# A hybrid decoder layer in split float32: queries in 512-column products, and layer norm by transposed moments

## The reference

```python
h = rmsnorm(x, g_mix[l]); proj = h @ w_in[l]          # 1024 x 4608
q, k, v = ...                                         # 8 heads of 64
u = proj[..., c_v:c_u] + b_glu[l]                     # 2 x 512 channels
o = moba_attention(q, k, v)                           # causal softmax, 256 keys
a, g = split(u); z = a * sigmoid(g)
z = depthwise_conv(z, w_dw, 31 taps) + b_dw           # 512 channels, causal
z = (z - mean(z)) * rsqrt(var(z) + EPS)               # over the 512 channels of a token
cz = silu(z * ln_g + ln_b)
merged = gate_a * (o @ w_attn_up[l]) + gate_c * (cz @ w_conv_pw[l] + b_conv_pw[l])
x = x + merged @ w_out[l]
h = rmsnorm(x, g_ffn[l])
x = x + square(relu(h @ w_ff1[l])) @ w_ff2[l]; return rmsnorm(x, g_final)
```

## Time and profile before

| | |
|---|---|
| median of three runs | 351.67 us |
| span of the profiled execution, first to last instruction | 350.3 us |
| TensorE busy | 344.2 us (98%) |
| TensorE weight loads | 289.5 us (83%) |
| VectorE busy | 251.5 us (72%) |
| ScalarE busy | 192.1 us (55%) |
| GpSimd busy | 3.5 us |
| read from memory | 63.0 MB, 183 GB/s over the span |

### The profile page before, as it was taken

How to read it: one execution, slowest core, us unless ns; L and a number is a source line. 1 busy time by engine, 2 the same in 40 slices (tenths; PEclk the granted TensorE clock), 3 DMA queues, 4 the chain that set the end, 5 groups by cost and what they waited for, 6 DMA issues and landing times.

```text
span 350.3 us, 4670 instructions
## 1 busy us (share of the span) xinstructions
PE 344.2 (98%) x1766; PEld 289.5 (83%) x1766; DVE 251.5 (72%) x313; ACT 192.1 (55%) x236; POOL 3.5 (1%) x13
## 2 busy tenths in 40 slices
PE   8999999999999999999999999999999999999994
PEld 5889988787778888888888888888888888889884
DVE  2969999899999889965666946639466394563813
ACT  4985644698796358434674535515355163551534
POOL 1000000000000000000000000000000000000000
PEclk9999999999999999999999999999999999999998
DMA  8999455534353365783647472944729537260003
GB/s 278 349 387 377 155 206 156 206 122 153 121 198 130 120 239 156 265 254 110 198 157 227 152 252 90 299 180 128 248 102 301 178 121 243 115 239 0 0 0 120
DMA packets 34429, 64.23 MB, mean 183 GB/s; under 512 B 1360, under 2 KB 6000, under 8 KB 34416
## 3 DMA queue, kind: packets, MB, share of 16 engines
q1 hardware_dynamic: 34056, 63.56, 54.0%
q10 hardware_dynamic: 360, 0.49, 0.4%
HBM read 63.00 MB, written 1.05 MB: 183 GB/s over the span
## 4 chain that ended last, share of the span: by engine, by line
PE 98%; DVE 0%; issue 0%; DVEq 0%; ACT 0%
PE ps L971 20%; PE ps L972 19%; PE ps L973 19%; PE ps L1230 17%; PE ps L1238 9%; PE ps L958 4%; PE ps L1018 2%; PE ps L1122 1%; PE ps L1121 1%; PE ps L1123 1%; PE ps L1029 1%; PE ps L1072 1%; PE ps L1097 1%; PE ps L998 1%; PE ps L1191 0%; PE ps L1282 0%
## 5 line engine op out<-in xcount | busy, mean ns | idle before, releaser
L971 PE MATMUL ps<-w_hi,a_lo 128*128 128x512 f32 x256 | 100.9, 394 | 0.0
L972 PE MATMUL ps<-w_hi,a_hi 128*128 128x512 f32 x256 | 99.8, 390 | 0.0
L973 PE MATMUL ps<-w_lo,a_hi 128*128 128x512 f32 x256 | 99.7, 390 | 0.0
L899 DVE TENSOR_TENSOR w_lo<-raw,w_hi 128x2048 fp32r<-128x2048 f32 x28 | 63.5, 2287 | 6.2 <-ACT w_hi L623 6.2
L405 ACT CAST w_hi<-raw 128x2048 fp32r<-128x2048 f32 (+1 forms) x30 | 53.7, 1799 | 19.9 <-PE ps L973 19.7
L1230 PE MATMUL ps<-b_both,w_hi 128*128 128x512 f32 x256 | 61.3, 390 | 0.0
L674 DVE TENSOR_TENSOR w_lo<-raw,w_hi 128x2048 fp32r<-128x2048 f32 x26 | 59.3, 2285 | 1.7 <-ACT w_hi L405 1.7
L623 ACT CAST w_hi<-raw 128x2048 fp32r<-128x2048 f32 x28 | 52.8, 1914 | 7.5 <-PE ps L973 7.5
L971 PEld LDWEIGHTS ps<-w_hi,a_lo 128*128 128x128 f32 x256 | 48.1, 188 | 10.1 <-issue 0.5
L973 PEld LDWEIGHTS ps<-w_lo,a_hi 128*128 128x128 f32 x256 | 48.0, 188 | 10.2
L972 PEld LDWEIGHTS ps<-w_hi,a_hi 128*128 128x128 f32 x256 | 48.1, 188 | 9.4
(11 more groups left out here) (138 smaller groups left out, 302.5 us busy)
## 6 DMA issues: line engine op xcount, KB each, us to landing
raw<-in_w_ff_dram SPq DMA_DIRECT2D x32, 1024.0 KB, 5.4
raw<-in_w_in_dram SPq DMA_DIRECT2D x14, 1024.0 KB, 5.9
raw<-in_w_out_dram SPq DMA_DIRECT2D x4, 1024.0 KB, 5.3
raw<-in_w_in_dram SPq DMA_DIRECT2D x14, 256.0 KB, 5.7
raw<-in_w_attn_up_dram SPq DMA_DIRECT2D x2, 1024.0 KB, 5.2
raw<-in_w_conv_pw_dram SPq DMA_DIRECT2D x2, 1024.0 KB, 5.1
res<-in_x_dram SPq DMA_DIRECT2D x2, 512.0 KB, 3.9
raw<-in_w_in_dram SPq DMA_DIRECT2D x4, 128.0 KB, 4.1
```

The lines of the kernel that those rows point to most:

```text
L899: nc.vector.tensor_tensor(w_lo[:, slot], raw[:, slot], w_hi[:, slot].bitcast(F32), ALU.subtract).then_inc(lo_made, 1)
L971: nc.tensor.matmul(dst, lo[:, tok], w_hi[:, slot, k], start=start, stop=False, skip_group_check=seeded)
L972: nc.tensor.matmul(dst, hi[:, tok], w_hi[:, slot, k], start=False, stop=False, skip_group_check=seeded)
L973: return nc.tensor.matmul(dst, hi[:, tok], w_lo[:, slot, k], start=False, stop=stop, skip_group_check=seeded)
```

## The change

**Queries.** `a_hi` and `a_lo` become the two halves of one tile `a_both`. For each channel chunk, four matmuls of 512 columns (high weight by both halves) replace eight of 256, and four of 256 (low weight by the high half) follow. ScalarE copies the cross half out (`q_cross`), and VectorE adds the other half to it (`queries_sum`, two additions of 512 columns) at its step 6, which now gives `q_made`.

**Taps.** Step 6 loses three of its nine taps, and a new step 16 has three.

**Layer norm.** `S_LN` goes from 16 to 17, and the transposes of `conv` move from behind unit 16 into unit 17, after its first 12 matmuls. `zn`, its two VectorE passes and its eight transposes are gone. TensorE instead transposes the means and inverse roots, each broadcast to 128 columns: four transposes in unit 18 after 6 matmuls, which leave both as rows of tokens on all partitions. VectorE then centres and scales `conv` where it lies, in four passes of 512 columns that read the moments from PSUM, and the sigmoid and the linear part read `conv` from SBUF.

```diff
-S_QSCALE, S_KT = 6, 8
+S_QSCALE, S_QSUM, S_KT = 6, 6, 8
-S_LN = 16
+S_LN = 17
...
-CONV_AT = {2: 6, 3: 12, 4: 9, 5: 9, 6: 9, 7: 7, 8: 6, 9: 5, 10: 8, 11: 11, 12: 12, 13: 11, 14: 10, 15: 5}
+CONV_AT = {2: 6, 3: 12, 4: 9, 5: 9, 6: 6, 7: 7, 8: 6, 9: 5, 10: 8, 11: 11, 12: 12, 13: 11, 14: 10, 15: 5, 16: 3}
...
+        def moment_row(m):
+
+            row = ps[:, SB0, m * T:m * T + T].rearrange("p (c t) -> p c t", c=1)
+            return row.to_broadcast([P, 2, T])
...
-                    nc.scalar.copy(qk_t[:, 0, 2 * half:2 * half + 2], ps[:, bank:bank + 2, 0:T]).then_inc(q_made, 1)
+                    nc.scalar.copy(qk_t[:, 0, 2 * half:2 * half + 2], ps[:, bank:bank + 2, T:2 * T]).then_inc(q_cross, 1)
...
                 if n == S_SILU:
+                    act.wait_ge(o_lo, 1)
                     for c in range(CC):
-                        act.wait_ge(zn_tr, 1)
-                        nc.scalar.activation(conv[:, c], chunks(SB0)[:, c], ACT.Sigmoid, bias=vec[:, V_LNB + c:V_LNB + c + 1],
+                        act.wait_ge(zc_made, c // 2 + 1)
+                        nc.scalar.activation(o_t[:, c], conv[:, c], ACT.Sigmoid, bias=vec[:, V_LNB + c:V_LNB + c + 1],
...
+            def queries_sum():
+
+                for half in range(2):
+                    bank = Q_BANKS[2 * half]
+                    dve.wait_ge(q_cross, half + 1)
+                    part = qk_t[:, 0, 2 * half:2 * half + 2]
+                    nc.vector.tensor_tensor(part, ps[:, bank:bank + 2, 0:T], part, ALU.add).then_inc(q_made, 1)
...
-                    dve.wait_ge(rstd_made, 2)
-                    for t in range(TT):
-                        nc.vector.tensor_scalar(zn[:, t], ps[:, TB + t], mean_var[:, t, 0:1], rstd[:, 1, t:t + 1],
-                                                ALU.subtract, ALU.mult).then_inc(zn_made, 1)
                 if n == S_SILU:
 
-                    dve.wait_ge(zn_tr, 1)
+                    dve.wait_ge(moments_tr, 1)
+                    for half in range(2):
+                        pair = slice(2 * half, 2 * half + 2)
+                        nc.vector.tensor_tensor(conv[:, pair], conv[:, pair], moment_row(0), ALU.subtract).then_inc(centred, 1)
+                        dve.wait_ge(centred, half + 1)
+                        nc.vector.tensor_tensor(conv[:, pair], conv[:, pair], moment_row(1), ALU.mult).then_inc(zc_made, 1)
+                    for half in range(2):
+                        dve.wait_ge(zc_made, half + 1)
+                        for c in (2 * half, 2 * half + 1):
+                            nc.vector.tensor_scalar(silu_x[:, c], conv[:, c], vec[:, V_LNG + c:V_LNG + c + 1],
+                                                    vec[:, V_LNB + c:V_LNB + c + 1], ALU.mult, ALU.add).then_inc(silu_lin, 1)
...
-                        dst = ps[:, Q_BANKS[c], 0:T]
-                        nc.tensor.matmul(dst, w_hi[:, n % SLOTS, k, cols], a_lo[:, kk], start=kk == 0, stop=False)
-                        nc.tensor.matmul(dst, w_hi[:, n % SLOTS, k, cols], a_hi[:, kk], start=False, stop=False)
-                        last = nc.tensor.matmul(dst, w_lo[:, n % SLOTS, k, cols], a_hi[:, kk], start=False,
-                                                stop=kk == KD - 1)
+                        nc.tensor.matmul(ps[:, Q_BANKS[c]], w_hi[:, n % SLOTS, k, cols],
+                                         a_both[:, kk].rearrange("p a t -> p (a t)"), start=kk == 0, stop=False)
+                    for k in range(HK):
+                        kk = HK * (n % 2) + k
+                        last = nc.tensor.matmul(ps[:, Q_BANKS[c], 0:T], w_lo[:, n % SLOTS, k, cols], a_hi[:, kk],
+                                                start=False, stop=kk == KD - 1)
...
+            def conv_transposed():
+
+                pe.wait_ge(conv_step, (TAPS - 1) * CC)
+                pe.wait_ge(ot_made, PAIRS)
+                for t in range(TT):
+                    for c in range(CC):
+                        last = transpose(ps[:, TB + t, c * P:c * P + P], conv[:, c, t * P:t * P + P])
+                last.then_inc(conv_tr, 1)
...
-                         (lambda: glu_transposed(GLU_AT[n])) if n in GLU_AT else None)
+                         (lambda: glu_transposed(GLU_AT[n])) if n in GLU_AT else conv_transposed if n == S_LN else None)
...
-            def zn_transposed():
-                pe.wait_ge(zn_made, 1 + TT)
-                transpose_chunks(SB0, lambda t, c: zn[:, t, c * P:c * P + P]).then_inc(zn_tr, 1)
+            def moments_transposed():
+
+                pe.wait_ge(stats_made, 1)
+                pe.wait_ge(rstd_made, 2)
+                for t in range(TT):
+                    transpose(ps[:, SB0, t * P:t * P + P], mean_var[:, t, 0:1].to_broadcast([P, P]))
+                for t in range(TT):
+                    last = transpose(ps[:, SB0, T + t * P:T + t * P + P], rstd[:, 1, t:t + 1].to_broadcast([P, P]))
+                last.then_inc(moments_tr, 1)
...
-                     zn_transposed if U_ATTN + col == S_SILU else None)
+                     moments_transposed if U_ATTN + col == S_SILU else None, place=1)
```

More of the change, by code:

```diff
@@ L257, in build @@
         cz_lo = sem("cz_lo")
+        q_cross = sem("q_cross")
         q_made = sem("q_made")
@@ L798, in _ @@
+                    for half in range(2):
[3 more added lines that the diff above has]
+                                                    vec[:, V_LNB + c:V_LNB + c + 1], ALU.mult, ALU.add).then_inc(silu_lin, 1)
                     for half in range(2):
                         dve.wait_ge(silu_sig, 2 * half + 2)
-                        for c in (2 * half, 2 * half + 1):
-                            nc.vector.tensor_scalar(silu_x[:, c], chunks(SB0)[:, c], vec[:, V_LNG + c:V_LNG + c + 1],
-                                                    vec[:, V_LNB + c:V_LNB + c + 1], ALU.mult, ALU.add).then_inc(silu_lin, 1)
@@ L1165, in _ @@
                     values(n - S_ATT - 2)
-                if n == S_LN:
-                    pe.wait_ge(conv_step, (TAPS - 1) * CC)
-                    pe.wait_ge(ot_made, PAIRS)
-                    for t in range(TT):
-                        for c in range(CC):
-                            last = transpose(ps[:, TB + t, c * P:c * P + P], conv[:, c, t * P:t * P + P])
-                    last.then_inc(conv_tr, 1)
-            def zn_transposed():
-                pe.wait_ge(zn_made, 1 + TT)
-                transpose_chunks(SB0, lambda t, c: zn[:, t, c * P:c * P + P]).then_inc(zn_tr, 1)
+            def moments_transposed():
[6 more added lines that the diff above has]
+                last.then_inc(moments_tr, 1)
             def merged_transposed(col, bank):
```

21 lines of the change are left out of this document (12 added, 9 removed).

## The result

The changed kernel takes 355.11 us (median of five, 354.28 to 355.87) against 351.67 before (five runs, 351.25 to 352.0): a ratio of 1.0097, 95% interval 1.0086 to 1.0109. It is 3.4 us slower. The forecast was 353.7 with a range of 353.0 to 355.3: the sign and the stated range held, and 1.4 us of the loss were not in the sum.

A forecast was written before the change was run, and what follows sets the result against it. TensorE bounds the kernel, busy 344.2 of 350.3 us. Span: 350.3 - 0.4 (queries) - 0.44 (transposes) + 2.75 (wait for taps) + 0.1 (restart) = 352.3; runs are 1.37 above the span: 353.7 us, range 353.0 to 355.3.

The forecast's parts named there:

- unit 20's wait: Rival: VectorE's chain from moments to bias is slower than priced, unit 20 starts 0.2 to 0.8 us late; 354.2 us; chance 0.07.
- a clock case: Rival: TensorE's clock halves after the wait for the taps; around 2 us likely, 2.9 at most; 355.7 us; chance 0.12.
- The taps: Unit 17: the last tap ends at 120.10, TensorE asks at 117.40; 2.75 us lost, from 2.4 to 3.0.
- The restart behind it: Refilling TensorE's pipeline after the wait for the taps: 0.1 us taken, between nothing and 0.3.
- The queries: Units 4 and 5 on TensorE: wider matmuls take 11.08 us instead of 11.49; gain 0.4 us, from 0.3 to 0.45.
- VectorE's additions: The queries' sum in step 6: starts near 50.6 us without waiting, ends 1.8 us before TensorE needs it; costs nothing.
- The transposes: Layer norm on TensorE: four transposes instead of `zn`'s eight; gain 0.44 us, from 0.3 to 0.5.
- a sign that the forecast itself had named for being wrong: The prediction is wrong if matmuls behind the wait for the taps come 0.4 us apart.
- The moments: Unit 18: GpSimd's root is there at 123.4 us, TensorE comes at 124.8; 1.4 us to spare.
- Unit 20: ScalarE's bias copies end at 134.6 us, 0.2 before unit 20 asks; costs nothing, up to 0.4 if PSUM passes are slower.

The follow-up runs named there:

- the kernel with the taps first: The changed kernel with the three taps of step 16 put ahead of `low(19)` instead of behind it: 353.64 us.
- the kernel with the queries alone: The kernel before with only the new queries, the taps' table and the layer norm as they were: 351.67 us, ratio 0.9997.
- the kernel with nothing but VectorE's wait: The changed kernel with one wait added: VectorE waits for GpSimd's inverse root before `low(20)`: 354.71 us.
- VectorE held at the root as well: The changed kernel with its last three taps in step 15 and VectorE waiting for GpSimd's root before `low(20)`: 351.98 us, ratio 1.0006.

## Why the prediction was right, and where it was not

**The number, right with luck.** The forecast of 353.7 had a range of its own, 353.2 to 354.3 (its high end adds up to 354.4), and 355.11 lies outside it. The stated range holds it only because it was widened to take in unit 20's wait, which did not come, and the milder half of a clock case given 0.12. And two losses that were not in the sum overlap: had the root not run beside the slow matmuls, 1.6 and 0.8 us on top of 353.7 would have been past 355.3.

**The taps, right.** The forecast was 2.75 us. Measured 2.76 by starts. It was the term that decided the sign, and the kernel with the taps first shows that `low(19)` ahead of them makes 2.2 of it. The restart behind it, taken at 0.1, is 0.07.

**The queries, right in kind.** 0.4 forecast, 0.30 measured in every kernel that has them: the lower end given. That changing width every four matmuls is what takes the 0.1 is the forecast's reason and was not tested. VectorE's additions waited for nothing; they started at 51.48, 0.9 later than forecast, and at 50.57 in the kernel with the queries alone.

**The transposes, right.** 0.44 forecast, 0.44 measured; a stationary operand that repeats one column is priced as any other.

**The clock, a rival that came true.** It stood at a chance of 0.12, "around 2 likely"; it happened in four executions of five and cost 1.60 us of matmul time, by a sign that the forecast itself had named for being wrong (matmuls 0.4 apart behind the wait). The price was near, the chance was not, and in those executions this is the 1.4 us missed. The argument against it, that TensorE had been busy for 100 us before and works again after under 3 us, did not hold. Nor was the clock full in every slice, as the forecast read: the last digit of the clock row is an 8, and in that trace the clock falls to half at 348.4 us, 3.0 us after the last matmul's end. The page of the Trainium skill quoted there spoke against the change, and the traces agree with its warning: the clock fell in the wake of idle times of 2.1 us and more, in most executions though not in all, and in none of the kernels in which they were filled or cut to 1.5 or less.

**The moments, the step that failed.** The forecast had the root 2.55 us behind the start of the statistics and 1.4 us ahead of TensorE. It took GpSimd's 0.70 us from the earlier trace rows and did not ask what VectorE does meanwhile. Before, VectorE sat idle beside the root, waiting for it:

```profile
119.22 1.53 DVE L793 TENSOR_SCALAR zn<-ps,mean_var,rstd 128x512 f32<-128x512 f32 x2 [0.81 <-POOL rstd L385]
```

The change took that wait away and put `low(20)` there. The root then takes 2.67 us and comes 4.53 behind the start of the statistics (121.08 to 125.61). So it is 0.6 us late for a TensorE at full clock, 0.8 by starts, and in the profiled execution this was hidden by the slow matmuls. With the root at 0.70 the forecast's margin is real: 1.3 us in the kernel with nothing but VectorE's wait. With the right size the sum for a full clock is 353.7 + 0.7 = 354.4, and the one such execution took 354.28; with the clock down it is 353.7 + 1.6 = 355.3, and the four took 354.96 to 355.87.

**Unit 20, right in the changed kernel.** It waits for nothing there: the bias copies end at 135.64 and unit 20 starts at 136.57, 0.9 us to spare where 0.2 was forecast, since the four linear passes took 1.38 us and not 1.9. The place was worth watching even so: with VectorE held at the root as well it was the next to make TensorE wait, 0.39 us.

## What to carry to other kernels

When a change takes away a wait, ask what the other engine was spared by it: here VectorE's idle 0.8 us beside a GpSimd instruction kept that instruction at 0.70 us. Where VectorE's queue is full, the order inside a step decides: three multiply-adds behind a 2.2 us subtraction stopped TensorE for 2.6 us, in front of it for 0.4, and a step earlier not at all. And a long wait of TensorE can be dearer than its length: those of 2.1 us and more brought the clock down in 14 of 20 executions, and those of 1.5 and less in none of 10. The kernel with two short waits, 1.9 us of idle time together, was 1.5 us faster than the one with a single wait of 2.6. Filling the gap kept the clock up, but won only 0.4 to 0.7 us, because the root came next.

## What the runs showed of the hardware

- A GpSimd operation on 128x2 elements took 0.70 us alone or beside VectorE passes with one operand in PSUM, and 2.67 us beside a VectorE subtraction of 2048 columns with both operands in SBUF that had started 0.17 us earlier; it ended 0.55 us after the subtraction.
- TensorE's granted clock fell to half in the wake of idle times of 2.1 us (three of five executions), 2.6 us (seven of eleven) and 4.6 us (four of four), and not of 1.2 or 1.5 us (none of five each). It fell 1.1 us after work had resumed in one trace and 2 us before it in another. Eight matmuls of 512 columns then came 0.43 us apart. In the program's first 4 us the profile's granted clock reads 1.00 although matmuls come 0.43 apart there as well, so the distance of starts is the surer sign.
- A wait costs TensorE more than the idle time that the profile lists: 2.76 us by starts for 2.60 listed, 0.76 for 0.60, and 0.5 for 0.19 at unit 20.
- The time of an execution is 1.7 to 2.0 us above its span, and executions of one kernel differ by about 1 us in their first 30 us, once by 4.
